# Latent attention of a streaming encoder step: side jobs behind each tile's own work, value products two tiles behind, cached step at the end of a head

## What is computed

```python
def mla_block(q_lat, q_rope, qpos, ckv, krope, kpos):
    s = (einsum('bqhc,bkc->bhqk', q_lat, ckv)
         + einsum('bqhr,bkr->bhqk', q_rope, krope)) * ((NOPE + ROPE_DIM) ** -0.5)
    mask = (kpos[None, :] // CHUNK) <= (qpos[:, None] // CHUNK)
    p = softmax(where(mask, s, NEG_INF), axis=-1)
    return einsum('bhqk,bkc->bqhc', p, ckv)
# q_lat = q_nope @ w_uk per head; o = o_lat @ w_uv per head; 16 heads, KV_LORA 128, NOPE 64, ROPE_DIM 32, DV 64
```

## Time and profile before

| | us |
|---|---|
| median of 3 runs | 1822.04 |
| lowest, highest | 1816.11, 1824.68 |
| the profiled execution, its own time | 1824.61 |
| its span, first to last instruction | 1822.8 |
| mean granted TensorE clock | 0.958 of full speed |
| latent attention within the span | about 1354 to 1696 |

### The profile page before, as it was taken

How to read it: one execution, slowest core, us unless ns; L and a number is a source line. 1 busy time by engine, 2 the same in 40 slices (tenths; PEclk the granted TensorE clock), 3 DMA queues, 4 the chain that set the end, 5 groups by cost and what they waited for, 6 DMA issues and landing times. The chain is left out here.

```text
span 1822.8 us, 34118 instructions
## 1 busy us (share of the span) xinstructions
PE 1658.0 (91%) x12822; PEld 1297.1 (71%) x12822; DVE 1263.3 (69%) x2750; ACT 806.9 (44%) x1777; POOL 227.2 (12%) x314
## 2 busy tenths in 40 slices
PE   4788999999999969989998989998969999999798
PEld 1575577778888847767776878787857677767687
DVE  2577577779988938778887646437437777777764
ACT  3447322221112137768873326312217677767321
POOL 2222000000001032010100000110024232220000
PEclk7799999999999979999998989999989999999899
DMA  8314247652333169998727533424242111111532
GB/s 315 79 39 108 85 128 208 197 168 95 96 106 112 50 164 247 236 215 218 197 92 254 225 130 105 127 61 135 69 107 58 29 29 31 35 29 45 186 123 96
DMA packets 212243, 229.26 MB, mean 126 GB/s; under 512 B 122265, under 2 KB 146433, under 8 KB 211058
## 3 DMA queue, kind: packets, MB, share of 16 engines
q1 hardware_dynamic: 205202, 207.17, 40.5%
q0 software_dynamic: 6880, 19.92, 2.9%
HBM read 169.72 MB, written 54.16 MB: 123 GB/s over the span
## 5 line engine op out<-in xcount | busy, mean ns | idle before, releaser
L905 PE MATMUL PS<-ab_wh,hT 128*128 128x512 f32 x576 | 231.6, 402 | 3.8 <-DVE ab_wl L1256 3.8
L906 PE MATMUL PS<-ab_wl,hT 128*128 128x512 f32 x576 | 226.1, 392 | 0.0
L907 PE MATMUL PS<-ab_wh,hT 128*128 128x512 f32 x576 | 225.5, 392 | 0.0
L1449 DVE TENSOR_SCALAR_CACHE_REDUCE topk_junk<-scores,topk_small 128x528 bf16<-128x528 f32 (+6 forms) x224 | 194.6, 915 | 1.3
L2661 DVE CUSTOM_DVE_ANT_0 la_S<-PS,la_mask 128x128 f32<-128x128 f32 (+3 forms) x144 | 107.5, 747 | 41.7 <-PE PS L907 28.5
L1214 ACT ACTIVATE ab_nat<-PS 128x512 f32<-128x512 f32 x54 | 32.2, 596 | 229.9 <-PE PS L907 229.9
L905 PEld LDWEIGHTS PS<-ab_wh,hT 128*128 128x128 f32 x576 | 108.6, 189 | 31.5 <-issue 5.8
L907 PEld LDWEIGHTS PS<-ab_wh,hT 128*128 128x128 f32 x576 | 108.5, 188 | 24.8
L906 PEld LDWEIGHTS PS<-ab_wl,hT 128*128 128x128 f32 x576 | 108.6, 189 | 21.5
L905 PE MATMUL PS<-out_wh,out_mT 128*128 128x512 f32 x288 | 116.2, 404 | 4.7 <-DVE out_mT L2111 4.7
L1808 ACT ACTIVATE at_P<-at_S,at_nm 128x128 f32<-128x128 f32 (+2 forms) x144 | 110.5, 767 | 16.7 <-DVE at_nm L1853 16.3
(11 more groups left out here) (428 smaller groups left out, 4223.6 us busy)
## 6 DMA issues: line engine op xcount, KB each, us to landing
ab_wl_raw<-in_ab_w_in SPq DMA_DIRECT2D x64, 256.0 KB, 5.1
spare<-in_ada_w SPq DMA_DIRECT2D x32, 512.0 KB, 4.1
out_g<-scratch_gates_nat SPq DMA_DIRECT2D x18, 512.0 KB, 5.3
at_vc<-in_cache_a_v SPq DMA_DIRECT2D x8, 1024.0 KB, 10.4
at_vc<-in_cache_b_v SPq DMA_DIRECT2D x8, 1024.0 KB, 5.5
scratch_qcT<-c_T SPq DMA_DIRECT2D x72, 96.0 KB, 2.0
mod_ada_w<-in_ada_w SPq DMA_DIRECT2D x6, 1024.0 KB, 10.4
c_wl_raw<-in_c_w_in SPq DMA_DIRECT2D x24, 256.0 KB, 5.9
```

The source lines that it names most:

```text
L905: nc.tensor.matmul(out, x[0], w[0], start=start, stop=False)
L906: nc.tensor.matmul(out, x[0], w[1], start=False, stop=False)
L907: return nc.tensor.matmul(out, x[1], w[0], start=False, stop=stop)
L1449: go(V.tensor_scalar(mark, x, limit, 0.0, op, ALU.add, accum_out=cnt[:, m:m + 1]), 0 if m == M - 1 else 1)
```

## The change

Five things are changed, all in `latent_attention`. The batch step stands behind tile 7 in all heads but the last, where it stands behind tile 2. The side jobs of steps from 0 on move from `early` into `amid`, which each engine (and the numbering `seq`) runs behind the step's own transposes, halves or exponentials instead of ahead of the scores; lat and kr move to tiles 3 and 7 of the head before. Value products of tiles are made at it - 2 instead of it - 1, those of the batch step stay at it - 1, and the copy to `mix` follows to it - 2. `PT` gets a third buffer. `xs` has two instead of three.

```diff
--- before.py
+++ after.py
@@ -2222,7 +2222,7 @@
     for g in range(HC):
         for i in range(QT):
             order.append(("head", g, i))
-            if i == (QT - 1 if g == 0 else 3):
+            if i == (2 if g == HC - 1 else QT - 1):
                 order.append(("batch", g, QT))
     N = len(order)
     place = {(kind, g, i): s for s, (kind, g, i) in enumerate(order)}
@@ -2236,7 +2236,7 @@
             return [(0, nk, P), (nk, 1, TS)]
         return [(a, min(4, i + 1 - a), P) for a in range(0, i + 1, 4)]
 
-    FIRST, END = -2, N + 1
+    FIRST, END = -2, max(N + 2, batch_at(HC - 1) + 5)
     early = {it: [] for it in range(FIRST, END)}
     for n, (kind, half) in enumerate((("k", 0), ("v", 0), ("k", 1), ("v", 1))):
         early[FIRST + n].append((kind, 0, half))
@@ -2249,14 +2249,17 @@
         early[n - 1].append(("uk", n, 0))
         early[n + 1].append(("ql", n, 0))
     for b in range(NB):
-        early[batch_at(2 * b) - 6].append(("lat", b, 0))
-        early[batch_at(2 * b) - 5].append(("kr", b, 0))
+        early[head_at(2 * b - 1, 3) if b else batch_at(0) - 6].append(("lat", b, 0))
+        early[head_at(2 * b - 1, 7) if b else batch_at(0) - 5].append(("kr", b, 0))
+    amid = {it: early[it] if it >= 0 else [] for it in early}
+    early = {it: early[it] if it < 0 else [] for it in early}
     late = {batch_at(HC - 1) + 3 + n // 2: [("o", m, 0) for m in (n, n + 1)] for n in (0, 2)}
     seq = []
     for it in range(FIRST, END):
         seq += early[it]
         if 0 <= it < N:
             seq += [("turn", it, j) for j in range(len(parts(it)))]
+        seq += amid[it]
         if 0 <= it - 2 < N and order[it - 2][0] == "batch":
             seq.append(("back", it - 2, 0))
         if 0 <= it - 1 < N and order[it - 1][0] == "batch":
@@ -2280,8 +2283,8 @@
         sb = lambda n, shape, dt=F32: stack.enter_context(nc.sbuf_tensor(f"la_{n}", shape, dt))
         q, k, v = sb("q", [P, 2, 2, SEQ], BF16), sb("k", [P, 2, 2, 2, SEQ], BF16), sb("v", [P, 2, 2, QT, 2 * DV], BF16)
         Ssb, Psb, mask = sb("S", [P, 2, SEQ]), sb("P", [P, 2, SEQ]), sb("mask", [P, SEQ])
-        PT, PTs = sb("PT", [P, 2, 2, QT, P], BF16), sb("PTs", [P, 2, nk + 1, P])
-        latT, u, us, xs = sb("latT", [P, 2, SEQ], BF16), front.x, sb("us", [P, 2, 2, HC * NOPE], BF16), sb("xs", [P, 3, 512])
+        PT, PTs = sb("PT", [P, 3, 2, QT, P], BF16), sb("PTs", [P, 2, nk + 1, P])
+        latT, u, us, xs = sb("latT", [P, 2, SEQ], BF16), front.x, sb("us", [P, 2, 2, HC * NOPE], BF16), sb("xs", [P, 2, 512])
         lat, kr3 = sb("lat", [P, 2, nk, KVL]), sb("kr3", [P, 2, nk, 3 * RD])
         latTs, krT = sb("latTs", [P, 2, 2, PAST], BF16), sb("krT", [3 * RD, 2, PAST], BF16)
         ql, qr = sb("ql", [P, 2, NB, HC, TS], BF16), sb("qr", [3 * RD, NB, HC, TS], BF16)
@@ -2380,13 +2383,13 @@
                     for d in range(2):
                         for h in range(2):
                             rows = slice(NOPE * h, NOPE * (h + 1))
-                            expand(k[rows, a % 2, h, d, cols], xs[rows, e % 3], k[rows, a % 2, h, 0, cols] if d else None)
+                            expand(k[rows, a % 2, h, d, cols], xs[rows, e % 2], k[rows, a % 2, h, 0, cols] if d else None)
                 else:
                     if a >= 2 and half == 0:
                         pool.wait_ge(valued, tiles_done(2 * a - 3, QT - 1))
                     hi, lo = (v[:, a % 2, d, 4 * half:4 * half + 4, :].rearrange("p a b -> p (a b)") for d in range(2))
-                    expand(hi, xs[:, e % 3])
-                    expand(lo, xs[:, e % 3], hi)
+                    expand(hi, xs[:, e % 2])
+                    expand(lo, xs[:, e % 2], hi)
                 if e == 3:
                     pool.wait_ge(sample_in, 16 * 11)
                     pool.wait_ge(expanded, n_op[0])
@@ -2493,7 +2496,7 @@
                     pe.wait_ge(resulted, g)
                 hs, cols = QT * g + i, slice(DV * (g % 2), DV * (g % 2 + 1))
                 for j in range(i + 1):
-                    last = product(nc, PS[:, 7, i * DV:(i + 1) * DV], [PT[:, hs % 2, d, j, :] for d in range(2)],
+                    last = product(nc, PS[:, 7, i * DV:(i + 1) * DV], [PT[:, hs % 3, d, j, :] for d in range(2)],
                                    [v[:, g // 2 % 2, d, j, cols] for d in range(2)], j == 0, j == i)
                 last.then_inc(valued, 1)
 
@@ -2526,20 +2529,20 @@
                         score_batch(s, g)
                 if 0 <= it < N:
                     turn_weights(it)
+                for job in amid[it]:
+                    unit(*job)
                 if 0 <= it - 2 < N and order[it - 2][0] == "batch":
                     turn_back(it - 2)
-                if 0 <= it - 1 < N:
-                    kind, g, i = order[it - 1]
-                    if kind == "head":
-                        value_head(it - 1, g, i)
-                    else:
-                        value_batch(it - 1, g)
+                if 0 <= it - 2 < N and order[it - 2][0] == "head":
+                    value_head(it - 2, *order[it - 2][1:])
+                if 0 <= it - 1 < N and order[it - 1][0] == "batch":
+                    value_batch(it - 1, order[it - 1][1])
                 for job in late.get(it, []):
                     unit(*job)
 
         def wait_staging(engine, e):
-            if e >= 3:
-                engine.wait_ge(expanded, wide_ops(e - 3))
+            if e >= 2:
+                engine.wait_ge(expanded, wide_ops(e - 2))
 
         by_batch = lambda n: PS[:, bank(n), :].rearrange("p (h b t) -> p b h t", h=4, b=NB)
         packed = lambda t, d, a: t[:, d, 4 * a:4 * a + 4, :].rearrange("p a b -> p (a b)")
@@ -2553,7 +2556,7 @@
                     if e % 2 == 0:
                         act.wait_ge(turned, n + 1)
                         wait_staging(act, e)
-                        nc.scalar.activation(xs[:, e % 3], PS[:, bank(n), :], ACT.Copy).then_inc(unit_free[n % 3], 1)
+                        nc.scalar.activation(xs[:, e % 2], PS[:, bank(n), :], ACT.Copy).then_inc(unit_free[n % 3], 1)
                     return
                 act.wait_ge(turned, n + 1)
                 if kind == "uk":
@@ -2585,8 +2588,8 @@
                 if 0 <= it < N:
                     kind, g, i = order[it]
                     hs = QT * g + i
-                    if kind == "head" and hs >= 2:
-                        act.wait_ge(valued, hs - 1)
+                    if kind == "head" and hs >= 3:
+                        act.wait_ge(valued, hs - 2)
                     if kind == "batch" and g >= 2:
                         act.wait_ge(turned, number["value", batch_at(g - 2), 0] + 1)
                     for j, (first, n, w) in enumerate(parts(it)):
@@ -2594,10 +2597,12 @@
                         src = PS[0:w, bank(m), 0:n * P]
                         if kind == "head":
                             act.wait_ge(turned, m + 1)
-                            nc.scalar.activation(PT[:, hs % 2, 0, first:first + n, :].rearrange("p a b -> p (a b)"), src, ACT.Copy).then_inc(high, 1)
+                            nc.scalar.activation(PT[:, hs % 3, 0, first:first + n, :].rearrange("p a b -> p (a b)"), src, ACT.Copy).then_inc(high, 1)
                         elif j == 1:
                             act.wait_ge(turned, m + 1)
                             nc.scalar.activation(PTs[0:w, g % 2, first:first + n, :].rearrange("p a b -> p (a b)"), src, ACT.Copy).then_inc(unit_free[m % 3], 1)
+                for job in amid[it]:
+                    unit(*job)
                 if 0 <= it - 1 < N and order[it - 1][0] == "batch":
                     l = order[it - 1][1]
                     m = number["value", it - 1, 0]
@@ -2622,7 +2627,7 @@
                     if e % 2 == 1:
                         dve.wait_ge(turned, n + 1)
                         wait_staging(dve, e)
-                        nc.vector.tensor_copy(xs[:, e % 3], PS[:, bank(n), :]).then_inc(unit_free[n % 3], 1)
+                        nc.vector.tensor_copy(xs[:, e % 2], PS[:, bank(n), :]).then_inc(unit_free[n % 3], 1)
                     return
                 if kind == "o":
                     dve.wait_ge(turned, n + 1)
@@ -2675,16 +2680,18 @@
                         if kind == "head":
                             m = number["turn", it, j]
                             after_high()
-                            hi, lo = (PT[:, hs % 2, d, first:first + n, :].rearrange("p a b -> p (a b)") for d in range(2))
+                            hi, lo = (PT[:, hs % 3, d, first:first + n, :].rearrange("p a b -> p (a b)") for d in range(2))
                             nc.vector.tensor_tensor(lo, PS[:, bank(m), 0:n * P], hi, ALU.subtract).then_inc(unit_free[m % 3], 1)
+                for job in amid[it]:
+                    unit(*job)
                 if 0 <= it - 2 < N and order[it - 2][0] == "batch":
                     l = order[it - 2][1]
                     m, b, hh = number["back", it - 2, 0], l // 2, l % 2
```

(4 more changed lines are left out.)

## The result

The changed kernel takes 1792.91 us (median of four runs, 1788.47 to 1795.53) against 1823.36 before (four, 1816.11 to 1828.22): a ratio of 0.985 (95% interval 0.983 to 0.987), 28 us less by the ratio and 30 by the medians. The forecast was 1797, its range 1786 to 1809.

A forecast was written before the change was run, and what follows sets the result against it. TensorE, nearest to full, stalls 4.63 us a pair of heads on VectorE's low halves; 4.63 - 1.1 = 3.5, over seven pairs 24.5, plus 0.5 for heads 0 and 1, tail 0: 25 off 1822.04 makes 1797 us, range 1786 to 1809.

The forecast's parts named there:

- The measure of the room: TensorE's stalls in a pair of heads: 4.63 us by count of gaps, 3.2 by matmul busy time.
- The walk: New order followed unit by unit from tile 7's scores: stalls of 0.6 (odd head), 0.3 (even), 0.2 (k, v units) stay.
- The bank ring: Three PSUM banks that units take in turn; named the new danger of moving side jobs behind.
- 3.02 us of the pair: Side jobs behind the tile's own work: stalls at latent block, v, k, kr units and one caused behind go.
- air: Batch step behind tile 7: its values give VectorE and ScalarE 1.4 us right after the wide tiles.
- the 1.61: Values two tiles behind: all stalls before values, 1.61 us in a pair, go.
- Heads 0 and 1 are nearly full: 0.5: Term of the sum for the stage's first two heads: 0.5 us gained there.
- The 0.08 us of the earlier trace: Head 0, batch already at its end: TensorE busy 14.22 of 14.30 us over wide tiles and batch.
- B: Rival: three banks still bind, wide stretches keep half their stalls; 16 us off, 1806; chance 0.21.
- C: Rival: all stalls go, as in head 0; 33 us off, 1789; chance 0.11.
- D: Rival: no gain, waits only handed on to exponentials or next transposes; 1822, within 9; chance 0.08.
- E: Rival: slower, side jobs' banks freed later, 7.4 us of stalls in a pair; 1841; chance 0.05.

The follow-up runs named there:

- sides_only: Kernel before with only the side jobs of steps from 0 on put behind their tile's own work; 1810.7 us, ratio 0.995.
- values_only: Kernel before with tile values two steps behind, three buffers of turned weights and xs of two; 1815.4 us, ratio 0.997.
- batch_only: Kernel before with the batch step behind tile 7 (last head: tile 2) and lat and kr moved to the head before; 1798.0 us, ratio 0.988.
- start_and_tail: Changed kernel with side jobs of its first five steps ahead again and the last two output units one step later; 1787.05 us, ratio 0.982.
- ring_of_two: Changed kernel with the units going round two PSUM banks instead of three; 1848.4 us, ratio 1.015.
- S: The part that puts side jobs behind the tile's own work; alone against the kernel before 39.12 us a pair, ratio 0.995.
- V: The part that makes tile values two steps behind; alone (with xs of two) against the kernel before 39.77 us a pair, ratio 0.997.

## Why the prediction was right, and where it was not

**The measure of the room held.** 4.63 us of stalls in a pair by the count of gaps, a floor of 35.73; measured 36.23, so 0.50 of stalls stay where I had 1.1 (bounds 0.3 to 2.3). The pair came out at 36.2, just below the 36.5 to 37.5 named as right. The seven pairs so gave 28.9 us where the sum had 24.5, and start and end took 2.4 where it had 0.5 gained: two errors, 4.4 and 2.9, that for the most part cancel. That the stage's 26.5 lies so near to the forecast 25 is luck; the pair itself came out within its bounds. By matmul busy time alone (3.2 us of room) the result would have been impossible: 4.13 went, since each stall also costs the 0.16 us of overlap. What the Trainium skill says of the two measures (Perfetto Trace Analysis, Identifying the Most-Contended Engine), that matmul busy time is a bad measure and the share of weight loads (with MFU, which was not computed here) a good one, this case bears out only in its first half: weight loads fill 28.55 of 36.22 us, 79%, while TensorE has 0.5 us left.

**The walk held, with too much left over.** It put the rest before the transposes of the wide tiles, and there the largest piece of it is; the timeline of TensorE, the odd head's tile 7:

```profile
1513.72 1.35 PE L2487 MATMUL PS<-ident,la_P 128*128 128x128 f32 x8
```

Eight transposes take 1.06 us where nothing holds them, so 0.29 is a slip between the two halves; in the even head 0.14 stands before the same transposes. The other gaps in the pair are of 0.1 or less. The walk had 0.6 and 0.3 for the two heads and 0.2 for k and v units; why it came out too high was not looked into. The bank ring was the right place to look, and I walked through it only in the new order.

**The division failed,** in the step "This removes the stalls before L2432 and before the v, k and kr units, and the one that the first causes: ... 3.02 us of the pair", and in the next but one, which gave the batch step "air" and no price. Both named for each stall the job that stood before the wait, not the unit that had taken the bank. sides_only gave 1.24 of the 3.02, values_only 0.58 of the 1.61; the stalls went on to the next unit. batch_only gave 3.31. Had I made the count n - 3 in the old order, the transpose back would have stood in it. One name was wrong too: the unit at 1509.38 is the key unit of tile 6, not a v unit (a v unit is twelve small matmuls); the sum is not touched. The start failed as well: "Heads 0 and 1 are nearly full: 0.5" gave no price to side jobs that stand behind their tile where the stage starts, and the four comparisons under start_and_tail put it at 1.5 to 2.1 us, with what the clock has in it.

**Head 0 had said so.** The 0.08 us of the earlier trace rows came with side jobs ahead and values one behind, with only the batch step in its new place. I used the row as a bound for the whole change and did not ask which of the three parts it had.

**Rivals.** B, three banks still bind, did not come: no steady wait for L2684 is left in the changed kernel. But the ring was what bound the kernel before, and ring_of_two shows that the margin is less than one bank. (The sentence of the Trainium skill that the prediction names for B stands in the same page's section Optimization Strategy; the kernel before and ring_of_two bear it out, the changed kernel shows that the same three banks can do.) C, all stalls gone, 33 us off, was nearly right inside the pairs, 4.13 of 4.63; start and end took 2.4 us of it. D, handed on, is in good part what S and V do alone: 1.78 of 3.02 and 1.03 of 1.61 did not come. E did not come.

**Terms.** SyncE's later loads and xs of two were hidden, as forecast: the changed kernel's waits in the stage name neither. The tail's wait for tile 7's low half is there (0.6 us), as forecast.

## What to carry to other kernels

Where an engine waits for a buffer of a ring, count back along the ring from the waiting unit: the cause is what takes the places between, which may be a small job of 0.27 us that never waits itself. Put such jobs where the others take one place a step, and check by moving only them. And a stretch of the same trace that shows no stall is an experiment already made: list what it has and the others have not.

## What the runs showed that I had not expected

Parts that each remove a wait do not add: 1.24 + 0.58 + 3.31 = 5.13 us alone, 4.13 together, and 0.30 + 0.51 + 1.91 = 2.72 as the last one (the 3.31 with the moved `lat` and `kr`, the 1.91 without). Code that is the same in all fourteen kernels put the start of the stage 13.6 us apart between single executions, while the stage's pairs repeat within 0.13 us. And a gap can be a record that is missing: only the weight loads beside it tell.
